# Routing of the two sparse tiles inside the expert blocks, pair lists beside the queries, packed gathers and one scan stage

## Chip, cores and metric

The kernel runs on one core of a Trainium2 chip. The metric is the device time of one execution in microseconds (us). Three runs of the kernel before took 5330.02, 5340.7 and 5357.9 us; their median is 5340.7.

## What is computed

Two layers of a decoder trunk, for 512 prompt tokens and 64 sample tokens (8 sequences of 8) that share all weights. In each layer the tokens pass a combined projection, three mixers (an RWKV-7 state, a gated delta net, a differential attention) and an output projection. Then comes the expert part, to which most of the change belongs:

```
q = (xb @ wq).reshape(TB, 8, 2, 128)
s = einsum('thcd,hcnd->thcn', q, keys)
sv, si = top_k(s, 16)
cand = sv[:, :, 0, :, None] + sv[:, :, 1, None, :]       # 16 x 16 pairs per head
tv, ti = top_k(cand, 16)                                  # 128 experts of 16384 per token
gate = softmax(tv)
act = gelu(einsum('td,tjd->tj', xb, u_tab[eidx]))
out = einsum('tj,tjd->td', gate * act, v_tab[eidx])
```

The scan that the change merges is the chunked recurrence of the two state mixers: per chunk of 64 tokens, corrections against the state, outputs, and an update of the state. The samples start from their own states, one per sequence.

## The kernel before

**Stages.** Each layer is a sequence of stages. A stage gives every engine its own list of instructions, ordered by semaphores, and ends with a barrier of all engines. All waits are written out by hand; an engine works its list strictly in order. A helper, `Steps`, counts results on a semaphore, and its `settle` (L142) waits for all of them. Tokens stand in five tiles: tile 0 (the first 128 prompt tokens), tiles 1 to 3 (the other 384) and the last tile (64 samples on 64 partitions).

**Scan (L1352 to L1410) and samples' scan (L1416 to L1487).** The prompt runs in eight chunks. In each, PE multiplies the state with 16 small products ("begins", L1365), DVE adds them into SA (L1387), PE makes the state's increment and the outputs ("ends", L1369 to L1377), and DVE scales and adds the state (L1390, L1392). Each kind of product alternates between two PSUM banks. The samples follow in a stage of their own: 128 products against their states (L1424), a turn (L1430), SA (L1465), outputs (L1435 to L1439), expansions by sequence (L1462, L1469), state increments (L1445, L1447) and additions (L1473, L1478), with a store of the states (L1483).

**Query stage (L1609 to L1699).** For each of 16 half-key lists PE makes queries and scores of all five tiles. ACT copies the scores out (L1673, L1674) into one of two buffers, and DVE takes the top 16 of each tile in five steps of five instructions (L1693 to L1697).

**Routing stage (L1732 to L1914).** The order of tiles is 0, last, 1, 2, 3. For each tile POOL adds the 16 x 16 candidates (L1829), DVE takes their top 16 for eight heads (L1859 to L1863), ACT makes the exponentials, and DVE looks up the two half indices by a comparison (L1880), a product on POOL (L1839) and a reduction (L1885). PE turns the result (L1753), ACT copies it out. Tiles 0 and last keep lists: the expert number and gate of every token and pair, for gathers ("sparse" tiles). For the 384 tokens of tiles 1 to 3 ("dense" tiles) the gates go into a table over all 16384 experts: per octet of eight tokens, DVE makes one-hots (L1849), ACT scales them (L1795), PE multiplies (L1768), ACT evicts (L1804), and SP stores the table to DRAM. One-hots of a tile are made between the steps of the next.

**Expert stage (L1966 to L2225).** It runs over 128 blocks of 128 experts. Per block: SP loads u and v (and a piece of the gate table for two blocks); ACT and DVE split u and v into two parts (L2009, L2142; L2015, L2146); PE makes hidden values of the 384 dense tokens (24 products, L153 to L155); ACT applies gelu (L2021); DVE multiplies with gates and splits (L2154 to L2160); PE multiplies with v into six PSUM banks (18 products, L2085). PE works on the hidden values of block b + 1 before the outputs of block b.

The sparse tokens ride along. POOL gathers one row of u per token and pair (`fetch_u`, L2046) into a ring of four buffers, and DVE makes a dot with the token's vector (`dot`, L2165): 128 gathers of 64 rows in blocks 0 to 39 for the samples, 128 gathers of 128 rows in blocks 40 to 82 for tile 0. Then gelu and gate, and 32 "summing" blocks each (47 to 78 and 89 to 120), in which POOL gathers rows of v (L2059), PE sums them (`half`, L2097) and DVE adds the result (L2174). The order of DVE's instructions in a block is written in the loop at the end of its list: v split of block b + 1, a dot, u split of block b + 2, a dot, the gate product of block b + 1, then the other dots.

```
LATE_DOTS, FIRST_DOTS = (0, 40), (40, 83)
LATE_SUMS, FIRST_SUMS = 47, 89
LATE_ACT, FIRST_ACT = 42, 84
```

Of the kernel before, what the change touches and what calls it, by code (L numbers as in the profile page):

```python
# [63 lines left out]
GAIN_AT = 20992  # L64
# [101 lines left out]
def trunk(nc, t):  # L166

    ctx = ExitStack()
    with ctx:
# [138 lines left out]
        with nc.Fori(0, DEPTH) as layer:  # L308
# [1043 lines left out]
            with stage(nc, "s_ready", "ws_done", "sa_ready", "out_done", "ds_done", "y_out", "scaled", "state_out", "s0_in") as (  # L1352
                    block, s_ready, ws_done, sa_ready, out_done, ds_done, y_out, scaled, state_out, s0_in):
                @block.tensor
                def _(pe):
                    for c in range(8):
                        tk = slice(c * CH, (c + 1) * CH)
                        bw, bo, bd = c % 2, 2 + c % 2, 4 + c % 2
                        at_ = lambda m, j: slice((m * 2 + j) * CH, (m * 2 + j + 1) * CH)
                        pe.wait_ge(s_ready, c + 1)  # L1360
                        if c >= 2:
                            pe.wait_ge(sa_ready, 2 * (c - 1))
                            pe.wait_ge(y_out, 2 * (c - 1))
                        for m, j, p in mh:
                            last = pe.matmul(ps[p, bw, at_(m, j)], tm(WT[m])[p, c, j], S[p, m, j], start=True, stop=True)  # L1365
                        last.then_inc(ws_done, 1)
                        pe.wait_ge(sa_ready, 2 * (c + 1))
                        for m, j, p in mh:
                            pe.matmul(ps[p, bd, at_(m, j)], tm(Kx[m])[p, c, j], SA[p, c % 2, m, j], start=True, stop=(m == 1))  # L1369
                            if m == 0:  # L1370
                                pe.matmul(ps[p, bd, at_(m, j)], tm(K_t)[p, c, j], tm(V_t)[p, c, j], start=False, stop=True)
                        for m, j, p in mh:
                            o = ps[p, bo, at_(m, j)]
# [5 lines left out]

                @block.vector  # L1380
                def _(dve):
                    dve.memset(S, 0.0).then_inc(s_ready, 1)
                    dve.wait_ge(s_ready, 1)
                    for c in range(8):
                        dve.wait_ge(ws_done, c + 1)
                        for m in range(2):
                            dve.tensor_tensor(SA[:, c % 2, m], tm(UU[m])[:, c], ps[:, c % 2, m * 128:(m + 1) * 128].rearrange("p (j n) -> p j n", j=2),  # L1387
                                              ALU.add).then_inc(sa_ready, 1)
                        dve.wait_ge(out_done, c + 1)
# [219 lines left out]
            with stage(nc, "keys_in", "wq_in0", "wq_in1", "hi_ready", "lo_ready", "q_done", "q_out", "s_done", "s_out", "v_steps", "ranked") as (  # L1609
# [15 lines left out]
                def _(pe):  # L1625
# [12 lines left out]
                    def scores(c):  # L1638
# [3 lines left out]
                        if c >= 2:  # L1642
                            pe.wait_ge(s_out, 2 * (c - 1))
# [679 lines left out]
```

## Time and profile before

| | us |
|---|---|
| median of three runs | 5340.7 |
| the profiled execution | 5362.85 |
| its span, first to last instruction | 5361.0 |
| PE busy | 4201.9 (78%) |
| DVE busy | 3266.7 (61%) |
| POOL busy | 1733.7 (32%) |
| ACT busy | 1467.0 (27%) |

The profile is of one execution. Busy shares are means over stages that have different limits, so the rows that follow later are cut by stage: layer 0 begins at 0, layer 1 at about 2695 us from the span's start. PE is TensorE, DVE VectorE, ACT ScalarE, POOL GpSimd, SP the engine that issues most DMAs; PEclk is the granted clock of PE as a part of full speed (0.50 is 1.2 GHz, 1.00 is 2.4 GHz).

### The profile page before, as it was taken

Reading aid. Unit: us, or ns where it says so; the run is one execution under the profiler, and the core shown is the slowest. Engines: PE = TensorE matmul, PEld = TensorE weight load, DVE = VectorE, ACT = ScalarE, POOL = GpSimd, SP = SyncE. Lnnn points to the kernel's source line nnn. Section 1 sums busy time; section 2 is a strip of 40 time slices with the busy share of each in tenths; the row PEclk is TensorE's granted clock in tenths of the full one; section 3 lists DMA queues with packets and bytes.
Section 4 is the critical chain, followed back from the end, with each engine's and each line's share of the span. In section 5 each row is a group of like instructions: output and inputs, shape, how many; then the busy total and the mean of one; then the engine's idle time right before and its main releaser. Section 6 shows DMA issues by size and latency. Waiting matters only on the chain. (4 is left out here: it accounts for less than half of the span.)

```text
span 5361.0 us, 79852 instructions
## 1 busy us (share of the span) xinstructions
PE 4201.9 (78%) x30618; PEld 3580.2 (67%) x30618; DVE 3266.7 (61%) x6218; ACT 1467.0 (27%) x2688; POOL 1733.7 (32%) x1020
## 2 busy tenths in 40 slices
PE   6966585814699999999978756758057999999998
PEld 6945475814688877877778545748056888778777
DVE  2064624689678878744421555247896888786444
ACT  2132201307622222222222222122075222222222
POOL 2200101222155587523222002012322545774331
PEclk9966777958899999999989667679589999999999
DMA  3120001202599999988721200011026999998885
GB/s 111 53 70 13 2 15 36 74 4 94 182 223 226 303 345 362 325 273 312 236 71 58 68 7 2 18 50 56 4 110 199 235 232 311 353 360 288 303 314 195
DMA packets 462508, 870.68 MB, mean 162 GB/s; under 512 B 224768, under 2 KB 280896, under 8 KB 458272
## 3 DMA queue, kind: packets, MB, share of 16 engines
q1 hardware_dynamic: 349600, 464.54, 28.2%
q0 software_dynamic: 112640, 402.71, 22.7%
q8 instruction: 150, 2.46, 0.2%
q14 instruction: 118, 0.97, 0.1%
HBM read 805.56 MB, written 61.58 MB: 162 GB/s over the span
## 5 line engine op out<-in xcount | busy, mean ns | idle before, releaser
L153 PE MATMUL ps<-x_split,w_split 128*128 128x384 f32 (+1 forms) x3104 | 1029.1, 332 | 117.1 <-DVE w_split L2142 66.5
L2085 PE MATMUL ps<-w_split,c_split 128*128 128x512 f32 x4608 | 1108.4, 394 | 1.0 <-DVE c_split L2160 1.0
L2085 PEld LDWEIGHTS ps<-w_split,c_split 128*128 128x128 f32 x4608 | 853.1, 188 | 277.8 <-issue 108.2
L155 PE MATMUL ps<-x_split,w_split 128*128 128x384 f32 (+1 forms) x3104 | 1008.4, 325 | 0.0
L154 PE MATMUL ps<-x_split,w_split 128*128 128x384 f32 (+1 forms) x3104 | 1007.8, 325 | 0.0
L153 PEld LDWEIGHTS ps<-x_split,w_split 128*128 128x128 f32 x3104 | 592.2, 191 | 243.1 <-issue 130.3
L2165 DVE CUSTOM_DVE_ANT_0 arena<-arena 64x1024 f32<-64x1024 f32 (+1 forms) x512 | 621.8, 1215 | 177.3 <-DMA arena<-pk_u_rows,arena 107.8
L154 PEld LDWEIGHTS ps<-x_split,w_split 128*128 128x128 f32 x3104 | 592.6, 191 | 4.0
L155 PEld LDWEIGHTS ps<-x_split,w_split 128*128 128x128 f32 x3104 | 592.0, 191 | 0.0
L2015 ACT CAST w_split<-arena 128x1024 fp32r<-128x1024 f32 x256 | 268.7, 1049 | 1080.4 <-PE ps L2085 1079.7
L2046 POOL DMA_INDIRECT arena<-pk_u_rows,arena x256 | 366.1, 1430 | 526.3 <-DVE arena L2165 352.1
L2059 POOL DMA_INDIRECT arena<-pk_v,rows_sb x256 | 263.7, 1030 | 505.2 <-PE ps L2097 441.8
L329 POOL TENSOR_TENSOR w_split<-arena,w_split 128x2048 fp32r<-128x2048 f32 (+1 forms) x54 | 245.7, 4555 | 532.3 <-ACT w_split L323 532.3
L2046 POOL DMA_INDIRECT arena<-pk_u_rows,rows_sb x256 | 364.8, 1425 | 152.1 <-DVE arena L2165 83.1
L2146 DVE TENSOR_TENSOR w_split<-arena,w_split 128x1024 fp32r<-128x1024 f32 x256 | 311.2, 1216 | 95.0 <-ACT w_split L2015 95.0
L1768 PE MATMUL ps<-arena 128*128 128x128 f32 x1536 | 224.8, 308 | 169.2 <-ACT arena L1795 169.0
L2174 DVE TENSOR_TENSOR x_sb<-x_sb,ps 64x512 f32<-64x512 f32 (+1 forms) x256 | 173.9, 679 | 282.1 <-PE ps L2097 282.1
L1768 PEld LDWEIGHTS ps<-arena 128*128 128x128 f32 x1536 | 206.9, 217 | 187.7 <-ACT arena L1795 187.6
L2021 ACT ACTIVATE arena<-ps 128x384 f32<-128x384 f32 x256 | 125.7, 491 | 749.8 <-PE ps L155 749.7
L1252 POOL TENSOR_TENSOR arena<-arena,cst 128x1152 f32<-128x1152 f32 x24 | 63.2, 2649 | 815.5 <-SPq L125 761.6
L153 PE MATMUL ps<-w_split,x_split 128*128 128x256 f32 x800 | 229.3, 287 | 114.6 <-POOL w_split L329 114.6
L2142 DVE TENSOR_TENSOR w_split<-arena,w_split 128x1024 fp32r<-128x1024 f32 x256 | 311.3, 1216 | 5.6 <-ACT w_split L2009 5.6
(367 smaller groups left out, 6564.2 us busy)
## 6 DMA issues: line engine op xcount, KB each, us to landing
arena<-pk_u SPq DMA_DIRECT2D x256, 512.0 KB, 8.4
arena<-pk_v SPq DMA_DIRECT2D x256, 512.0 KB, 6.5
g_scratch<-arena SPq DMA_DIRECT2D x24, 2048.0 KB, 6.3
arena<-g_scratch SPq DMA_DIRECT2D x128, 384.0 KB, 9.1
arena<-w_in SPq DMA_DIRECT2D x28, 1024.0 KB, 5.4
arena<-pk_wq SPq DMA_DIRECT2D x16, 1024.0 KB, 6.5
arena<-cache_k SPq DMA_DIRECT2D x32, 256.0 KB, 2.7
arena<-cache_v SPq DMA_DIRECT2D x32, 256.0 KB, 3.5
```

The costliest lines, as they stand in the source:

```text
L153: pe.matmul(out, lhi, rhi, start=(n == 0), stop=False)
L154: pe.matmul(out, lhi, rlo, start=False, stop=False)
L155: last = pe.matmul(out, llo, rhi, start=False, stop=(n == len(terms) - 1))
L329: pool.tensor_tensor(w_part(s, 1)[:, :, 0:width], raw[:, s, :, 0:width], w_part(s, 0)[:, :, 0:width].bitcast(F32), ALU.subtract).then_inc( ...
L1768: last = pe.matmul(ps[:, 4 + 2 * (s % 2) + k // 4, (k % 4) * P:(k % 4 + 1) * P], ABs[s][:, 0, k], ABs[s][:, 1, k], start=True, stop=True)
L2015: act.copy(vs[:, s, 0], v_raw[:, s]).then_inc(v_hi, 1)
L2046: pool.indirect_dma_start(u_got[r, n % RING], None, u_rows, bass.IndirectOffsetOnAxis(ap=rowid[i][r, j:j + 1], axis=0)).then_inc(f_u[n % R ...
L2059: pool.indirect_dma_start(v_got[:, q % 2, g], None, v_rows, bass.IndirectOffsetOnAxis(ap=rowid_t[LATE if q < 32 else 0][:, tok:tok + 1], a ...
L2085: done = pe.matmul(ps[:, 1 + 2 * j + n, :], c_of[hc], vs[:, s, hv, n * 512:(n + 1) * 512], start=first and m == 0, stop=last and m == 2, s ...
L2142: dve.tensor_tensor(us[:, s, 1], u_raw[:, s], us[:, s, 0].bitcast(F32), ALU.subtract).then_inc(u_ready, 1)
L2146: dve.tensor_tensor(vs[:, s, 1], v_raw[:, s], vs[:, s, 0].bitcast(F32), ALU.subtract).then_inc(v_ready, 1)
L2165: dve.tensor_tensor_reduce(out=u_got[r, n % RING], in0=u_got[r, n % RING], in1=near_x[i][r], scale=1.0, scalar=0.0, op0=ALU.mult, op1=ALU. ...
```

## The change

- **Scan.** The samples' stage is gone. Its PE work stands in pieces between "begins" and "ends" of chunks 1 and 3 to 7; DVE's and ACT's pieces stand in the same chunks. The prompt's products use one bank of each kind instead of two, and PE waits for ACT's copy (`y_out`) before each chunk's outputs.
- **Query stage.** Only the three dense tiles are ranked. ACT copies the raw scores of tile 0 and the last tile into a buffer that is kept (`kept`). DVE takes the top 16 pairs of the dense tiles here, one head behind, in 18 rounds instead of 16.
- **Routing stage.** Only dense tiles remain, with the exponentials, shifts and casts of all three in one instruction each. The products of the lookups are on DVE; POOL has no work in the stage. The load of the gain row moves to the expert stage's SP list.
- **Expert stage.** DVE routes the last tile in blocks 0 to 15 and tile 0 in blocks 13 to 28, one part per block after the block's own work. near_x (the sparse tokens' normalised vectors) is made in block 6. SP copies the upper half of the samples' lists and their vectors to partitions 64 to 127 (three DMAs behind the loads of blocks 18 and 19), so that 64 gathers of 128 rows serve the samples. POOL waits for both tiles' numbers and for this copy before its first gather. Dots run in blocks 30 to 48 (64) and 49 to 88 (128), sums in 55 to 86 and 95 to 126.

The diff, cut to its core:

```diff
+                    begins(0)
+                    ends(0)
+                    begins(1)
+                    s_against_states()
+                    ends(1)
+                    begins(2)
+                    ends(2)
+                    begins(3)
+                    s_turned()
+                    ends(3)
...
+                    begins(7)
+                    s_states(1)
+                    ends(7)
...
-                            act.copy(SC[:, d % 2, 0:4], ps[:, 4 + 2 * (d % 2), :].rearrange("p (i n) -> p i n", i=4)).then_inc(s_out, 1)
-                            act.copy(SC[0:SAMP, d % 2, 4], ps[0:SAMP, 5 + 2 * (d % 2), 0:P]).then_inc(s_out, 1)
+                            act.copy(SC[:, d % 2], ps[:, 4 + 2 * (d % 2), 0:3 * P].rearrange("p (i n) -> p i n", i=3)).then_inc(s_out, 1)
+                            act.copy(kept[0][:, d], ps[:, 4 + 2 * (d % 2), 3 * P:4 * P]).then_inc(s_out, 1)
+                            act.copy(kept[LATE][0:SAMP, d], ps[0:SAMP, 5 + 2 * (d % 2), 0:P]).then_inc(s_out, 1)
...
+                    for c in range(18):
+                        h = (c - 2) // 2
+                        if c < 16:
+                            dve.wait_ge(s_out, 3 * c + 1)
+                        for step in range(5):
+                            if c < 16:
+                                half_keys(c, step)
+                            if h >= 0 and step < 3:
+                                pairs(h, step + 3 * (c % 2))
                             st.settle()
...
+                    for n in range(3):
+                        if n >= 1:
+                            dve.wait_ge(t_out, n)
+                        for c in range(2):
+                            st.did(dve.tensor_tensor(look[c].rearrange("p h j a -> p (h j) a"), bc(C("iota")[:, 0:TOPK], 1, P),
+                                                     bc(TAf[:, c, n], 2, TOPK), ALU.is_equal))
+                            onehots(n - 1, 2 * c, 2)
                         st.settle()
                         for c in range(2):
+                            st.did(dve.tensor_tensor(look[c], look[c], bc(SIf[:, n, :, c], 2, TOPK), ALU.mult))
+                            onehots(n - 1, 4 + 2 * c, 2)
+                        st.settle()
                         for c in range(2):
+                            last = dve.tensor_reduce(route[:, c, n], look[c].rearrange("p h j a -> p (h j) a"), AX.X, ALU.add)
+                            if c == 0:
+                                st.did(last)
+                        last.then_inc(route_ready, 1)
+                        onehots(n - 1, 8, 8)
+                    dve.wait_ge(t_out, 3)
+                    onehots(2, 0, 16)
...
+            SPARSE = (LATE, 0)
+            ROUTE_AT = (0, 13)
+            DOTS_AT = ((30, 49), (49, 89))
+            DOTS_OF = (P // 2, P)
+            SUMS_AT = (55, 95)
+            ACT_AT = (50, 90)
...
+                    sp.wait_ge(pack_ready, 1)
+                    lower, upper = slice(0, SAMP), slice(SAMP, P)
+                    sp.dma_start(near_x[LATE][upper], near_x[LATE][lower]).then_inc(packed, 16)
+                    sp.dma_start(rowid[LATE][upper, 0:SAMP], rowid[LATE][lower, SAMP:P]).then_inc(packed, 16)
+                    sp.dma_start(near_gate[LATE][upper, 0:SAMP], near_gate[LATE][lower, SAMP:P]).then_inc(packed, 16)
...
+                            if b == ROUTE_AT[k] + 10:
+                                act.wait_ge(k_shifted, k + 1)
+                                act.activation(k_ex[rows_of[i]], k_ex[rows_of[i]], ACT.Exp).then_inc(k_exp, 1)
...
+                    pool.wait_ge(k_routed, 2)
+                    pool.wait_ge(packed, 48)
...
+                    def routing(k, part):
+                        i = SPARSE[k]
+                        r = rows_of[i]
+                        w = r.stop
+                        if part < 4:
+                            for step in range(5):
+                                for c in range(4 * part, 4 * part + 4):
+                                    best_of(kept[i][r, c], k_SV[r, c], k_SI[r, c], step)
+                                nr.settle()
+                        elif part == 4:
...
+                        elif part < 9:
+                            for step in range(5):
+                                for h in range(2 * part - 10, 2 * part - 8):
+                                    best_of(k_pairs[0][r, h], k_TV[r, h], k_TI[r, h], step)
+                                nr.settle()
...
+                            if 0 <= b - ROUTE_AT[k] <= 15:
+                                routing(k, b - ROUTE_AT[k])
```

Parts 4 to 15 of `routing`, each in its own block: the pair sums and a cast (4), the pairs' top 16, two heads a block (5 to 8), subtraction, shifts and a cast (9), the two comparisons (10), products (11), reductions and the expert numbers (12), gates (13), and the turned numbers (15). PE's loops are split at the two turns. Each gather and dot now covers all 128 partitions.

## Rows read from the trace of the kernel before

**Rows 1.** Busy time by stage: length, PE, PEld, DVE, ACT, POOL, PEclk, DMA share, GB/s

```profile
763.00:807.00 44.00, 33.47 (x320) 29.06 (x320) 9.25 (x16) 0.81 (x3) 0.00 (x0) 0.58 0.07 27
...
967.00:1107.50 140.50, 126.68 (x928) 121.95 (x928) 100.92 (x640) 35.46 (x70) 27.55 (x6) 0.95 0.17 53
1107.50:1426.00 318.50, 115.41 (x783) 105.40 (x783) 265.15 (x438) 165.77 (x491) 77.22 (x15) 0.74 0.19 81
...
1438.00:1787.00 349.00, 325.67 (x1594) 293.67 (x1594) 281.06 (x431) 95.70 (x115) 172.33 (x120) 0.98 1.02 228
1787.00:1867.00 80.00, 80.00 (x408) 72.77 (x406) 70.17 (x111) 24.65 (x30) 43.24 (x33) 1.00 0.99 327
1867.00:2217.00 350.00, 342.92 (x1603) 248.53 (x1602) 277.31 (x449) 79.71 (x96) 271.52 (x158) 1.00 0.99 355
...
3773.50:4092.00 318.50, 115.47 (x783) 105.43 (x783) 265.14 (x438) 165.77 (x491) 77.21 (x15) 0.74 0.19 81
...
4104.00:4455.00 351.00, 335.09 (x1662) 303.95 (x1663) 293.05 (x450) 99.92 (x120) 177.22 (x124) 0.98 1.00 237
```

**Rows 2.** Timeline of ACT in the expert stage: gelu of blocks in succession

```profile
1460.49 0.49 ACT L2021 ACTIVATE arena<-ps 128x384 f32<-128x384 f32 x1 [2.12 <-PE ps L155]
...
1468.80 0.49 ACT L2021 ACTIVATE arena<-ps 128x384 f32<-128x384 f32 x1 [2.13 <-PE ps L155]
...
2310.88 0.49 ACT L2021 ACTIVATE arena<-ps 128x384 f32<-128x384 f32 x1 [3.31 <-PE ps L155]
...
2321.55 0.49 ACT L2021 ACTIVATE arena<-ps 128x384 f32<-128x384 f32 x1 [3.31 <-PE ps L155]
```

**Rows 3.** Waits of DVE, 1438 to 1787 us: total us, times, longest

```profile
DVE arena L2165 <- DMA arena<-pk_u_rows,arena: 60.2, 45, 4.0
```

**Rows 4.** Timeline of the scan and the samples' scan: start, length, idle before

```profile
730.25 0.48 PE L1369 MATMUL ps<-arena 64*64 64x64 f32 x4 [0.66 <-DVE arena L1387]
...
761.45 0.42 DVE L1392 TENSOR_TENSOR S_sb<-S_sb,ps 128x256 f32<-128x256 f32 x1
...
765.04 1.29 DVE L1462 TENSOR_TENSOR arena<-arena,cst 128x512 f32<-128x512 f32 x2 [3.17 <-PEq L129]
...
802.24 0.35 SPq L1483 DMA_DIRECT2D o_state_s<-arena  x1
```

**Rows 5.** Busy time by window, inside the samples' scan

```profile
785.00:791.50 6.50, 6.50 (x79) 6.50 (x80) 0.00 (x0) 0.00 (x0) 0.00 (x0) 0.50 0.00 0
```

**Rows 6.** Timeline of DVE in the query stage: starts of two lists

```profile
1062.13 1.06 DVE L1693 MAX8 arena<-arena 128x8 f32<-128x128 f32 x5 [1.36 <-ACT arena L1674]
...
1069.95 1.06 DVE L1693 MAX8 arena<-arena 128x8 f32<-128x128 f32 x5 [1.37 <-ACT arena L1674]
```

**Rows 7.** Timeline of DVE in the routing stage, tile 1, and at its end

```profile
1186.22 2.70 DVE L1859 MAX8 arena<-arena 128x8 f32<-128x256 f32 x8
...
1201.11 0.42 DVE L1863 FIND_INDEX8 arena<-arena 128x8 uint32<-128x256 f32 x1
...
1202.49 4.49 DVE L1880 TENSOR_TENSOR arena<-cst,arena 128x2048 f32<-128x2048 f32 x2
1211.37 2.29 DVE L1885 TENSOR_REDUCE arena<-arena 128x128 f32<-128x2048 f32 x1 [4.38 <-POOL arena L1839]
...
1426.32 2.47 DVE L2186 SCALAR_TENSOR_TENSOR arena<-x_sb,small,arena 128x1024 f32<-128x1024 f32 x2 [19.68 <-PEq L129]
```

**Rows 8.** Groups of ACT, 1361 to 1419 us, the last dense tile: busy us, mean ns

```profile
L1795 ACT ACTIVATE arena<-arena 128x128 f32<-128x128 f32 x128 | 39.5, 418 | 2.8 <-DVE arena L1849 2.8
L1804 ACT COPY arena<-ps 128x512 f32<-128x512 f32 x32 | 17.4, 602 | 1.7 <-PE ps L1768 1.7
```

**Rows 9.** The page's costliest groups: the dots, busy us, mean ns

```profile
L2165 DVE CUSTOM_DVE_ANT_0 arena<-arena 64x1024 f32<-64x1024 f32 (+1 forms) x512 | 621.8, 1215 | 177.3 <-DMA arena<-pk_u_rows,arena 107.8
```

**Rows 10.** DMA issues, 1430 to 1790 us and 1790 to 1860 us: us to landing

```profile
arena<-pk_u_rows,arena POOLq DMA_INDIRECT x123, 9.2
...
arena<-pk_u_rows,rows_sb POOLq DMA_INDIRECT x22, 7.8
```

More of the change, by code:

```diff
@@ L63 @@
 NEAR_AT = 22784
-GAIN_AT = 20992
+KEPT_AT = 18176
 X_AT = 14 * SLOT + TILES * 3 * C_W
@@ L1354, in _ @@
                 @block.tensor
                 def _(pe):
-                    for c in range(8):
-                        tk = slice(c * CH, (c + 1) * CH)
[L1358 to L1366, printed above, removed]
+                    at_ = lambda m, j: slice((m * 2 + j) * CH, (m * 2 + j + 1) * CH)
@@ new lines, in _ @@
+                    begins(0)
[8 more added lines that the diff above has]
+                    ends(3)
+                    begins(4)
+                    s_outputs(0)
+                    ends(4)
+                    begins(5)
+                    s_outputs(1)
+                    ends(5)
@@ L1736, in trunk @@
                 g_saved = (g_saved0, g_saved1)
-                def of_octets(i, first, n):
-                    return range(i * P // OCT - GO + first, i * P // OCT - GO + min(first + n, octets(i))) if i not in near else ()
-                def lookup(n, c, r):
-                    return cands[n % 2 if c == 0 else 2][r]
+                PER = P // OCT
                 @block.tensor
@@ new lines, in _ @@
+                    act.wait_ge(shifted, 1)
+                    act.activation(ex, ex, ACT.Exp).then_inc(exp_done, 1)
+                    routes_out(0)
+                    for n in range(3):
+                        for m in range(PER):
+                            gated(n * PER + m)
+                            if m:
+                                evicted(n * PER + m - 1)
+                        evicted(n * PER + PER - 1)
+                        if n < 2:
+                            routes_out(n + 1)
@@ L1998, in _ @@
                     loads(1, 1)
-                    with sp.Fori(0, BLOCKS // 4 - 1) as i:
+                    sp.dma_start(near_x[0], t["ffn_row"][L].broadcast_to([P, D])).then_inc(row_in, 16)
+                    with sp.Fori(0, 4) as i:
                         for s in range(2):
                             loads(i * 2 + (2 + s), s)
+                    sp.wait_ge(pack_ready, 1)
[3 more added lines that the diff above has]
+                    sp.dma_start(near_gate[LATE][upper, 0:SAMP], near_gate[LATE][lower, SAMP:P]).then_inc(packed, 16)
+                    with sp.Fori(0, BLOCKS // 4 - 5) as i:
+                        for s in range(2):
+                            loads(i * 2 + (10 + s), s)
                 @block.scalar
```

547 lines of the change are left out of this document (282 added, 265 removed).

## The prediction

> **What bounds the kernel now.** I read three things in this order: busy time by stage, to see which engine is full where; the order of instructions at the borders of the stages that the change touches; and the block period of the expert stage, for what happens if work is put there.
>
> By stage [rows 1], layer 0: the samples' scan holds 44 us, of which PE is busy 33.5. The query stage holds 140.5 us with PE busy 126.7: PE bounds it. The routing stage holds 318.5 us with PE at 115 and DVE at 265, so DVE sets it, with ACT taking over at its end. Layer 1's routing stage is as long. In the expert stage PE is nearly full. A plain block takes 8.31 us and a block that also sums a quad of sparse tokens 10.66 to 10.67 [rows 2], set by PE. PE idles where dots run: 23.3 us in blocks 0 to 41 of layer 0 (349 less 325.7), 15.9 in layer 1, and 7.1 in the first 32 summing blocks (350 less 342.9). The wait that ends last there is the u gather, 60.2 us of DVE waiting in 45 waits [rows 3]: a dot that waits for its gather delays the next u split, which PE wants. So of the change's four parts, one shortens a stage that DVE bounds, and the others shift work among stages that PE bounds.
>
> The sum is made against the profiled execution: span 5361.0 us, 5362.85 with what lies around it. That is 22 us above the median of the three runs, 5340.7. The prediction is the median less the sum, and 22 us go into the range. A run of this kernel can tell about 0.5% (27 us) from no change.
>
> **Scan merged.** Removed per layer: a stage border and the samples' own chain. From the end of the last state update of the prompt (761.45 + 0.42) to the issue of the samples' state store at 802.24 are 40.4 us [rows 4]; 3.2 of them pass before the first work. Added: the same PE work, about 34 us (33.5 busy in [rows 1], little of it outside this), now queued on PE between the "begins" and "ends" halves of seven chunks. There PE idles 0.66 us waiting for DVE's SA [rows 4], so 6 x 0.66 = 4 us of it is covered and some 30 is not. DVE's expansions stand before waits for PE in the same chunk and are covered by the inserted PE work; the last four state additions, 2.5 us, stay at the end. New: 30 + 2.5 = 32.5 for 40.4: **-8 us**. The new wait of PE for y_out (outputs now have one bank) and for the states' load come after a whole chunk: nothing. Bounds: 0 if the covers fail, -25 if the inserted 33.5 us ran at twice the clock (17 less). On that: at 785 to 791.5 us PE was busy the whole time and yet had a granted clock of 0.50 [rows 5], the 1.2 GHz level, so denser work of this shape brought no clock there. The Trainium skill (TensorE: Matmul & The Clock Gate, "What's actually happening") says that the throttled clock is the default and that activity releases it. By that rule the filled scan would run at 2.4 GHz and give up to 25 us per layer instead of 8; the row speaks against it, and I keep 8.
>
> **Pair lists beside the queries.** Before, DVE does 25 top-8 instructions per half-key list on five tiles: 1069.95 less its idle 1.37 less 1062.13, or 6.45 us, and then waits for ACT, that is PE; the period is 7.82 us [rows 6]. After: 15 of these (0.258 each, 3.9 us) and, for each head, so every second list, 15 instructions on 256 wide. Forty of those took 1186.22 to 1201.53, 0.383 each [rows 7], so 5.7, and an addition over 768 elements of 0.9 (2048 take 2.25). That is 3.3 per list. DVE's total is 7.2, still under 7.82, so PE keeps the pace. The end grows: the last two lists come together, 2 x 0.75 more, and the last head has no cover, 6.6. **+8 us**. Bounds: +5 if the last head overlaps better, +16 if DVE's added waits make it slower than PE by 0.5 a list. ACT copies three pieces rather than two, inside its idle time.
>
> **Routing stage.** Removed: both sparse tiles, all pair top-k, and POOL's products and the waits for them (4.38 before one reduce [rows 7]). The dense lookups stay, with the products moved to DVE. Step by step: exponentials, shifts and casts for three tiles at once, 4.6 (an estimate from 128-wide operations near 0.25); first tile's lookups, 2 x 2.25 (compare) + 2 x 2.25 (product, taken like the compare) + 2 x 2.28 (reduce) = 13.5; a hand-over through PE and ACT, between 1 and 5, taken as 3. Then ACT paces: 128 scalings and 32 evictions take 39.5 + 17.4 us for 16 octets [rows 8], pipelined some 3.4 per octet. While DVE makes the next tile's six lookup operations between eight one-hots it supplies only one per 4 us (6 x 2.25 + 8 x 2.27 = 31.7), so the ninth octet starts at 34 and the tile ends at 34 + 8 x 3.4 + 3 = 64. Twice that is 128; the last tile is 2.3 + 16 x 3.4 + 3 = 60; the last store of the gate table and the border take 8. Sum 4.6 + 13.5 + 3 + 128 + 60 + 8 = 217 for 318.5: **-101 us**. Bounds: -114 if ACT never starves (58 per tile), -84 if the hand-overs take 6 more each. Gain row and near_x leave this stage at no gain: near_x, 2.47 us [rows 7], ran while the first u load was on its way.
>
> **Routing in the blocks.** Each sparse tile costs DVE per block: four blocks of 20 narrow top-8 (5.2), one of 2.6, four of 20/2 wide ones (3.8), one of 1.2, then 4.5, 4.5, 5.2, 1.2 and 0.4; near_x in block 6, 2.5. Together 115 us with the waits between steps some 10 more. DVE's own work is 3.7 us a block (70.17 busy in 9.6 blocks [rows 1], less 28.7 dots at 1.22 [rows 9]), so 29 blocks offer 29 x 4.6 = 133. It fits on the average; in the blocks of 5.2 it runs over by 0.6 to 1. The u split is made about 4.8 us before PE wants it (an estimate from the order of the block), so a backlog of that size is free: loss 3 us, between 0 and 12. Waits added: ACT for the subtraction before Exp (behind it the v and u casts; done a block earlier), PE for the row numbers before one transpose (hidden products behind it; two blocks of margin), SP for the pack (u and v loads behind it; ready when SP arrives, since SP stands three blocks later), POOL for routing and pack (only gathers behind it, first needed in block 30).
>
> **Dots.** 64 packed gathers of 128 rows replace 128 of 64 rows, in blocks 30 to 48 (3.37 a block), then 3.2 a block in 49 to 88, before 2.98. Landing takes 9.2 us for 64 rows and 7.8 for 128 [rows 10], so packing costs nothing per gather and saves 64. The blocks to 41 lose their 19.6 us of PE idle (mean of 23.3 and 15.9). The new ones: u, v, gate and 3.37 gathers are 3.01 MB a block. At 327 GB/s DMA was 0.99 busy with no PE idle, and 355 was the most sustained [rows 1]; so 8.5 to 8.9 us a block, 3 to 11 for the 19 blocks; I take 8 and 1 for the next six. Summing blocks carry 3.97 MB, 11.2 us at 355: 0.5 x 32 = 16 where 7.1 was lost. The Trainium skill (DMA: Bandwidth & Descriptors, "Where 436 GB/s comes from") puts a core's HBM side at about 358 GB/s. By that figure the 19 blocks would lose 2 rather than 8, an estimate; the rows' 327 to 355 decide. Balance: 3 + 8 + 1 + 16 = 28 for 26.7, less 3 for the first gate load, which no longer shares DMA with gathers: **-2**, between -22 and +25.
>
> Per layer -8 + 8 - 101 - 2 = -103, for two layers -206: 5340.7 - 206 = **5135 us**.
>
> **Rivals.** (a) DVE's backlog and gather waits eat the blocks: the blocks at their upper bound (27 more a layer) and the routing stage at -84 (17 more): -103 + 44 = -59 a layer, 5223. For it: 25 short steps in blocks of 8.31; against: the average fits. 0.12. (b) The scan takes the higher clock, -17 more a layer, by the rule named above: 5101. Against it stands [rows 5]. 0.10. (c) The routing stage does not give what it should: the dense tiles hand over as slowly as now. Then only the two sparse tiles leave, some -75 for the stage: 5340.7 - 2 x 77 = 5187. For it: ACT waits for one-hots at each tile already. 0.10. (d) Slower: routing instructions in the blocks take over twice the time, because each of the waits between steps costs DVE its pipeline. Price: 58 blocks x what exceeds 4.6; above 8.1 a block (computed 4.1 on average) the 206 are gone; at 8.6 the time is 5135 + 58 x 4 = 5367. Against: 25 such steps took 6.45 us with their waits [rows 6]. 0.03. Forecast as summed: 0.65.
>
> **Numbers.** Low: bounds of scan, stage and blocks combined, -30 a layer: 5075. High: to case (c) and into (a): 5205. Faster by over 0.5%: all but (d) and some mishap of measurement, 0.96; within 0.5%: 0.02; slower 0.02.
>
> **What would show it.** Right: routing stage near 217 us, query stage near 148, samples' work inside a scan of 84; blocks 0 to 28 at 8.31 with few longer ones; dots from block 30 with DVE waiting on gathers. Wrong: a routing stage over 240, block periods over 8.8 in blocks 0 to 28, query lists over 7.82.

## The result, and the profile after

The changed kernel takes 5089.2 us (median of four runs, 5086.4 to 5093.1); the kernel before, run beside it on the same chip, 5349.3 (5330.0 to 5370.2). The ratio is 0.9498, with a 95% interval of 0.9474 to 0.9522. The forecast was 5135 us, in a range of 5075 to 5205. The profiled execution spans 5091.2 us, 269.8 less than that of before, where the sum had 206.

Busy time by window, changed kernel, by stage as in [rows 1] (length, PE, PEld, DVE, ACT, POOL, PEclk, DMA share, GB/s): the scan with the samples inside, the query stage and the routing stage, in layer 0 and then in layer 1; then blocks 0 to 29, 30 to 54 and the first summing blocks of layer 0.

```profile
708.32:785.02 76.70, 59.02 (x961) 54.26 (x961) 19.91 (x50) 4.09 (x19) 0.00 (x0) 0.68 0.08 31
...
944.52:1095.39 150.87, 127.73 (x928) 122.99 (x928) 115.61 (x584) 36.36 (x86) 27.62 (x6) 0.92 0.16 50
1095.39:1303.02 207.63, 107.08 (x777) 98.22 (x777) 150.62 (x74) 163.04 (x485) 0.00 (x0) 0.87 0.29 122
...
3238.96:3314.13 75.17, 57.30 (x961) 52.46 (x961) 19.90 (x50) 4.09 (x19) 0.00 (x0) 0.72 0.09 31
3473.64:3623.07 149.43, 126.26 (x928) 121.53 (x928) 115.68 (x585) 36.37 (x86) 27.59 (x6) 0.92 0.16 50
3623.07:3830.33 207.26, 108.35 (x777) 99.46 (x777) 150.53 (x74) 162.91 (x485) 0.00 (x0) 0.86 0.29 122
...
1315.00:1563.00 248.00, 246.41 (x1245) 223.65 (x1246) 224.57 (x574) 80.44 (x97) 2.94 (x3) 1.00 0.51 153
1563.00:1770.00 207.00, 205.18 (x1034) 185.30 (x1033) 182.23 (x281) 61.34 (x75) 110.27 (x80) 1.00 0.99 349
1770.00:2040.00 270.00, 262.35 (x1219) 191.44 (x1217) 215.03 (x349) 61.82 (x75) 213.01 (x127) 0.98 0.99 357
```

The same stretches of the kernel before, the two scan stages together (layers 0 and 1) and the query stage:

```profile
711.94:807.43 95.49, 70.10 (x961) 62.97 (x961) 20.15 (x50) 4.28 (x19) 0.00 (x0) 0.59 0.07 25
967.43:1107.80 140.37, 126.60 (x928) 121.86 (x928) 100.93 (x641) 35.46 (x70) 27.57 (x7) 0.95 0.17 54
3374.82:3473.17 98.35, 72.94 (x960) 65.60 (x961) 20.15 (x49) 4.28 (x19) 0.00 (x0) 0.55 0.07 24
```

From these, and from the first gelu to the last of each expert stage, the ledger per layer (mean of both):

| part | predicted | measured |
|---|---|---|
| scan | -8 | -21.0 (-18.8, -23.2) |
| query stage | +8 | +9.8 (+10.5, +9.0) |
| routing stage, 318.5 us before | -101 | -111 |
| expert blocks, first gelu to last, with the first gate load | -2 | -16.8 (-21.8, -11.7) |
| sum | -103 | -139 |

Twice the sum is 278 us. Eight come back outside these parts: the last sums now run to block 126 and the time after the last gelu grows from 23.2 to 25.8 us, and the stages between the two layers take some more.

The routing stage by groups (busy, mean ns, idle before and what ended it), layer 0:

```profile
L1831 ACT ACTIVATE arena<-arena 128x128 f32<-128x128 f32 x384 | 118.0, 409 | 15.6 <-DVE arena L1864 15.6
L1864 DVE TENSOR_TENSOR arena<-cst,arena 128x2048 f32<-128x2048 f32 x48 | 108.0, 2287 | 23.9 <-PE ps L1814 12.0 <-ACT arena L1825 11.9
L1814 PE MATMUL ps<-arena 128*128 128x128 f32 x768 | 105.5, 296 | 74.7 <-ACT arena L1831 74.7
...
L1840 ACT COPY arena<-ps 128x512 f32<-128x512 f32 x96 | 51.9, 592 | 4.7 <-PE ps L1814 4.4 <-issue 0.2
```

PE waits for ACT's scalings alone (74.7 us), and ACT's own scalings and evictions wait for others only 20 us in all: ACT sets the stage, as forecast. One scaling takes ACT 118.0 / 384 = 0.31 us.

Gelu in the first summing blocks, timeline of ACT:

```profile
1773.71 0.49 ACT L2039 ACTIVATE arena<-ps 128x384 f32<-128x384 f32 x1 [2.13 <-PE ps L155]
1782.03 0.49 ACT L2039 ACTIVATE arena<-ps 128x384 f32<-128x384 f32 x1 [2.13 <-PE ps L155]
1799.40 0.49 ACT L2039 ACTIVATE arena<-ps 128x384 f32<-128x384 f32 x1 [10.04 <-PE ps L155]
```

The period of 8.31 [rows 2] holds, to 0.1 us, from the second block on in all but three of the first 30. Nearly all that the expert stage still loses lies in blocks 55 to 86, 19 us in layer 0 and 16 in layer 1, in a few long blocks like this one of 17.4 instead of 10.64. In fourteen traced layers whose expert stage is the same code these blocks lost 9 to 26 us, and the blocks from first gelu to last took 1213 to 1233 us: a difference of a few us between two single layers says nothing.

### The profile page after: what moved, and what is told of

Same layout as the page of the kernel before. It is cut to its first block and busy times, and to the rows that moved or that the text cites. A ratio compares the mean times of both kernels' runs of the same rounds, so it can differ in the third digit from the quotient of the medians.

```text
span 5091.2 us, 79448 instructions
## 1 busy us (share of the span) xinstructions
PE 4157.7 (82%) x30616; PEld 3540.1 (70%) x30616; DVE 3136.0 (62%) x5966; ACT 1473.9 (29%) x2720; POOL 1363.4 (27%) x862
## 5 line engine op out<-in xcount | busy, mean ns | idle before, releaser
L2197 DVE CUSTOM_DVE_ANT_0 arena<-arena 128x1024 f32<-128x1024 f32 x384 | 467.0, 1218 | 106.7 <-DMA arena<-pk_u_rows,rows_sb 81.2
L2066 POOL DMA_INDIRECT arena<-pk_u_rows,arena x128 | 174.7, 1365 | 1179.1 <-DVEq L2262 1025.7
L2066 POOL DMA_INDIRECT arena<-pk_u_rows,rows_sb x256 | 376.8, 1472 | 153.8 <-DVE arena L2197 96.1
L1814 PE MATMUL ps<-arena 128*128 128x128 f32 x1536 | 212.3, 297 | 147.8 <-ACT arena L1831 147.8
L1814 PEld LDWEIGHTS ps<-arena 128*128 128x128 f32 x1536 | 195.6, 207 | 165.1 <-ACT arena L1831 165.1
L2116 PE MATMUL ps<-arena 128*32 128x512 f32 x1536 | 275.0, 610 | 25.0 <-DVE x_sb L2270 22.5
```

The costliest lines, as they stand in the source:

```text
L1814: last = pe.matmul(ps[:, 4 + 2 * (s % 2) + k // 4, (k % 4) * P:(k % 4 + 1) * P], ABs[s][:, 0, k], ABs[s][:, 1, k], start=True, stop=True)
L2066: pool.indirect_dma_start(u_got[:, n % RING], None, u_rows, bass.IndirectOffsetOnAxis(ap=rowid[i][:, j:j + 1], axis=0)).then_inc(f_u[n % R ...
L2116: done = pe.matmul(ps[32 * g:32 * g + 32, 7, :], spread[:, s, g], v_got[:, s, g, n * 512:(n + 1) * 512], start=True, stop=True, skip_group ...
L2197: dve.tensor_tensor_reduce(out=u_got[:, n % RING], in0=u_got[:, n % RING], in1=near_x[i], scale=1.0, scalar=0.0, op0=ALU.mult, op1=ALU.add ...
```

## Experiments

All are edits of the changed kernel. Base: 5089.2 us, expert blocks 1223.7 and 1222.3 us from first gelu to last.

**The scan put back.** Edit: the two scan stages of before in place of the merged one.

> The changed kernel with the scan of before put back: the prompt's eight chunks in one stage, the samples in a stage of their own. Theory: what the two traces show between the state's memset and the next stage's first work (95.5 to 76.7 us in layer 0, 98.35 to 75.2 in layer 1) belongs to the merge, so 42 us come back: 5131 us (5125 to 5137), with both scan stages together at 95 to 98 us per layer. Rival: the merge itself is worth the 8 us per layer of the prediction and the rest came with something else (where the stage starts, the clock that the stage before leaves): 5105.

Measured: 5125.1 us (5115.4 to 5139.9), ratio to before 0.9563 (0.9528 to 0.9597). Both scan stages together take 98.4 us in each layer, at a mean granted clock of 0.55 in layer 0:

```profile
710.50:808.90 98.40, 73.00 (x960) 65.60 (x961) 20.17 (x49) 4.28 (x19) 0.00 (x0) 0.55 0.06 24
```

The merge is worth 36 us by the medians, at the lower end of the theory's range, and 45 by the scan's own windows, not 16: the theory. (The other 9 lie within what the expert blocks vary.) PE's work is the same list of products, but its busy time is 73.0 us apart and 57 to 59 merged. So 15 of the 22 us per layer are not covered idle time but a higher clock. The idle time of PE goes from 25.4 to 17.7 us, about the 8 that the prediction had.

**The wide products last.**

```diff
                     begins(6)
-                    s_states(0)
                     ends(6)
                     begins(7)
-                    s_states(1)
                     ends(7)
+                    s_states(0)
+                    s_states(1)
```

> The changed kernel with the samples' state products (512 columns each) moved from chunks 6 and 7 behind the last chunk. Theory: it is these products that bring the granted clock to 1.00 in chunks 6 and 7. Without them these chunks go back to 0.50 to 0.60 and take about 6.7 us each instead of 7.1 and 5.4 with the products inside, and the products stand bare at the end, 5 us at the higher clock and 10 at the lower: the scan grows by some 9 us a layer, 5107. Rival: the clock does not hang on them, the chunks run at 1.00 anyway (4.9 us as the first chunk) and only the idle time that the products covered comes back: 3 us a layer, 5095.

Measured: 5090.8 us (5087.5 to 5104.2), ratio 0.9501 (0.9469 to 0.9533): the rival's time. The scan took 82.7 and 76.1 us, where sixteen scans of kernels that leave it alone took 68.6 to 79.3, mean 75.7; so some 4 us more per layer, less than those scans differ among themselves. The clock did fall in the two chunks, as the theory has it, and in layer 1 too. First the changed kernel (716 to 724 us: PE on the products of 8 columns; 764 to 772: chunk 6 with the products of 512 columns), then this run (chunks 6 and 7 without them):

```profile
716.30:724.30 8.00, 8.00 (x107) 8.00 (x108) 0.00 (x0) 0.00 (x0) 0.00 (x0) 0.50 0.01 2
764.30:772.30 8.00, 7.03 (x114) 4.57 (x116) 2.68 (x7) 0.43 (x2) 0.00 (x0) 1.00 0.01 2
```

```profile
764.00:770.80 6.80, 5.13 (x101) 4.66 (x97) 2.54 (x7) 0.61 (x4) 0.00 (x0) 0.75 0.01 2
771.25:777.50 6.25, 5.11 (x82) 4.90 (x84) 2.11 (x6) 0.01 (x1) 0.00 (x0) 0.50 0.00 0
```

The clock follows these products; their place is worth little, since at the end they still find the higher clock for most of their 6.3 us.

**Fillers, four and two.** With reps 2 and then 1:

```diff
+                    def filler():
+                        for r in range(reps):
+                            for hf in range(2):
+                                p = slice(64 * hf, 64 * hf + 64)
+                                pe.matmul(ps[p, 7, :], C("id64")[p], cst[p, 0:512], start=True, stop=True)
...
                     begins(1)
+                    filler()
```

and the same behind begins(2) to begins(5). The fillers compute nothing that is used.

> The changed kernel with four more products of 64 x 512 on constants, into a bank that nothing reads, behind the state products of each of chunks 1 to 5: work that computes nothing, 1.7 us per chunk at the higher clock and 3.4 at the lower, 0.66 of it in time in which PE waits anyway. Theory: wide products keep the clock at 1.00 in chunks 1 to 5, whose products (about 42 us of them at 0.50 to 0.66) then take some 20 us less, and the fillers cost 1.1 x 5: 12 to 14 us less per layer, 5063. Rival: the clock stays at 0.50 and the fillers are bare cost, 2.8 x 5 per layer: 5117.

Measured: 5085.2 us (5078.3 to 5091.4), ratio 0.9485 (0.9455 to 0.9514), between the two and not clear of the base. The scan took 76.3 us in both layers, with PE busy 59 as without fillers, at a mean clock of 0.81.

> As the run with fillers in chunks 1 to 5, with two products of 64 x 512 per chunk instead of four (0.86 us at the higher clock, of which 0.66 lies in a wait of PE). The first run gave a granted clock of 0.96 to 1.00 through chunks 3 to 5 and a scan as long as without fillers (76.3 us): what the clock gave, the fillers took. Theory: half the filler keeps the clock as well, and costs 0.2 instead of 1.1 per chunk: a scan of 70 to 72 us, 5 us less per layer, 5080. Rival: half is too little to hold the clock, the scan stays at 74 to 77: 5089.

Measured: 5076.9 us (5072.8 to 5078.3), ratio 0.9462 (0.9439 to 0.9485), scans of 68.8 and 69.0 us: the theory. The whole scan, and two stretches in chunks 3 and 5:

```profile
705.85:774.68 68.83, 51.83 (x981) 43.67 (x981) 19.89 (x50) 4.08 (x19) 0.00 (x0) 0.84 0.10 35
727.00:735.00 8.00, 7.03 (x166) 5.68 (x163) 1.33 (x4) 0.43 (x2) 0.00 (x0) 0.91 0.01 2
751.00:759.00 8.00, 7.03 (x132) 4.86 (x130) 2.53 (x6) 0.60 (x3) 0.00 (x0) 1.00 0.01 2
```

More work on PE, and PE is busy 51.8 us instead of 57 to 59. In the sixteen scans without fillers PE idles 17.7 to 17.9 us, and all of their spread is its busy time: 50.9 us at a mean clock of 0.79 up to 61.6 at 0.65. So PE's clock sets the length of the scan. The order of work moves this clock but does not decide it alone: the same code without fillers reached 68.6 us once, as short as the two scans here.

**POOL takes scalings.** Three of an octet's eight (n), then two; PE waits for `b_pool` as well before an octet's products:

```diff
-                        for k in range(OCT):
+                        for k in range(OCT - n):
                             b = ABs[o % NAB][:, 1, k]
                             last = act.mul(b, b, routeT[:, 2, o * OCT + k:o * OCT + k + 1])
...
+                        for k in range(OCT - n, OCT):
+                            b = ABs[o % NAB][:, 1, k]
+                            last = pool.tensor_scalar(b, b, routeT[:, 2, o * OCT + k:o * OCT + k + 1], None, ALU.mult)
+                        last.then_inc(b_pool, 1)
```

> The changed kernel with three of each octet's eight scalings in the routing stage on POOL, which has no work there, instead of ACT. Theory: ACT sets the pace of the octets (3.29 us: eight scalings and two evictions), DVE is next with 2.27 a one-hot. With five scalings left ACT needs about 2.6: the last tile takes 47 us instead of 57, the first two 58 instead of 62, 18 us a layer, 5053. Rival: DVE or PE paces the octets with ACT only close behind, or POOL's scalings take longer than ACT's: no gain, 5089 or more.

Measured: 5140.4 us (5132.6 to 5146.8), ratio 0.9583 (0.9554 to 0.9613): 51 us slower, the rival's side. Groups of the stage, layer 0:

```profile
L1863 POOL TENSOR_SCALAR arena<-arena 128x128 f32<-128x128 f32 x136 | 177.0, 1323 | 90.8 <-DVE arena L1874 90.8
L1815 PE MATMUL ps<-arena 128*128 128x128 f32 x720 | 112.2, 328 | 87.5 <-POOL arena L1863 83.9 <-ACT arena L1832 3.6
```

PE's wait has gone over from ACT to POOL, whose scaling takes 1.32 us.

> The changed kernel with two of an octet's eight scalings on POOL. The run with three showed 1.32 us for one on POOL, where ACT takes 0.31, so that POOL set the pace with 4.0 us per octet and PE and DVE waited for it. Theory: with two POOL takes 2.65 and ACT 6 x 0.31 + 1.09 = 2.95, so ACT sets the pace again, at 2.95 instead of 3.29: 5 us less in the last tile and 1 to 2 in each of the others, 8 us per layer, 5073. Rival: a chain of one-hot, two POOL scalings and eight products per buffer of four holds the octets, no gain: 5089.

Measured: 5118.0 us (5113.6 to 5125.1), ratio 0.9543 (0.9508 to 0.9578): still 29 us slower than the base, so this theory fell too. POOL's scaling was 1.5 us here, and PE waited 69.5 us for POOL and 13.7 for ACT:

```profile
L1863 POOL TENSOR_SCALAR arena<-arena 128x128 f32<-128x128 f32 x96 | 142.8, 1505 | 114.0 <-DVE arena L1874 114.0
L1815 PE MATMUL ps<-arena 128*128 128x128 f32 x768 | 111.1, 308 | 83.2 <-POOL arena L1863 69.5 <-ACT arena L1832 13.7
```

Two of 1.5 and the step from the one-hot to POOL make more than ACT's 3.29 per octet; this sum was not tested by itself. Both runs agree that the scalings set the stage, and ACT is the faster place for them. A run with one on POOL was not made.

**How full DVE is in blocks 0 to 28.**

```diff
+                            if k == 0 and b < 29:
+                                for x in range(8):
+                                    dve.max_index(near_h[0].bitcast(U32)[:, 8 * x:8 * x + 8], C("iota")[:, 0:8], C("iota"))
                             if 0 <= b - ROUTE_AT[k] <= 15:
```

> The changed kernel with eight more index searches over 128 elements (0.26 us each, 2.06 together, results unused) on DVE in each of blocks 0 to 28. Theory: DVE has 8.31 - 3.7 = 4.6 us per block for routing and a free backlog of about one split's lead (4.8 us), and the routing as it stands uses this up almost wholly (DVE busy 8.06 of 8.31 in blocks 1 to 8, 0.7 us lost in each of blocks 18 and 19). So nearly all of the 29 x 2.06 = 60 us shows: by the sum of the parts 41 to 55 us per layer, 5170 to 5200. Rival: the blocks still have room, and less than a third shows: below 5130.

Measured (one run): 5177.5 us, 88 more than the base; the expert blocks take 46.5 and 41.2 us more, and blocks 20 to 23 have periods of 10.1 to 10.2 us. (Blocks 18 and 19 of that text are counted 17 and 18 below.) The theory holds: of 60 us added per layer, 50 and 48 show in blocks 1 to 29, so some 10 were free. In the changed kernel itself DVE runs over in silence: its v splits in blocks 1 to 3 start 9.04 us apart while PE keeps 8.31, because the split comes long before PE wants it.

```profile
1327.34 1.22 DVE L2179 TENSOR_TENSOR w_split<-arena,w_split 128x1024 fp32r<-128x1024 f32 x1
...
1336.38 1.23 DVE L2179 TENSOR_TENSOR w_split<-arena,w_split 128x1024 fp32r<-128x1024 f32 x1
...
1345.41 1.23 DVE L2179 TENSOR_TENSOR w_split<-arena,w_split 128x1024 fp32r<-128x1024 f32 x1
```

**Samples unpacked.** Rows of 64 partitions throughout, no copies, and:

```diff
-            DOTS_OF = (P // 2, P)
+            DOTS_OF = (P, P)
...
-                            pool.indirect_dma_start(u_got[:, n % RING], None, u_rows,
-                                                    bass.IndirectOffsetOnAxis(ap=rowid[i][:, j:j + 1], axis=0)).then_inc(f_u[n % RING], 16)
+                            r = rows_of[i]
+                            pool.indirect_dma_start(u_got[r, n % RING], None, u_rows,
+                                                    bass.IndirectOffsetOnAxis(ap=rowid[i][r, j:j + 1], axis=0)).then_inc(f_u[n % RING], 16)
```

> The changed kernel with the samples' u rows fetched as before, one token slot at a time: 128 gathers and 128 dots of 64 rows in blocks 30 to 48 instead of 64 of 128 rows, with no copies to partitions 64 to 127. Theory: a gather costs its turn of the ring of four and its dot whatever its rows are. By DVE alone 128 x 1.22 + 19 x 3.7 = 226 us stand in blocks that hold 158, 68 us more per layer; by the ring alone (9.2 landing, 1.2 dot, 0.6 to the next issue, four at a time) 128 gathers take 352 us, 194 more. So 5225 to 5480, and by the ring 5477. Rival: the bytes are the same and DMA sets the pace, so it stays at 5089.

Measured (one run): 5376.3 us. In the 19 blocks that the new order leaves to the samples' dots, unpacked rows undo the whole change: 287 us, 138 per layer in the expert blocks (1360.7 and 1361.5). It lies between DVE's bound and the ring's. Groups of DVE from 1575 to 1875 us, where blocks take 15 us:

```profile
L2189 DVE CUSTOM_DVE_ANT_0 arena<-arena 64x1024 f32<-64x1024 f32 (+1 forms) x131 | 158.5, 1221 | 70.8 <-DMA arena<-pk_u_rows,arena 70.2
```

**Dots behind the block's work.**

```diff
-                        for d in dots[0:1]:
-                            dot(*d)
...
-                        for d in dots[1:2]:
-                            dot(*d)
...
-                        for d in dots[2:]:
+                        for d in dots:
                             dot(*d)
```

> The changed kernel with all dots of a block behind the block's own work in DVE's order (after the v and u splits, the gate product and the sum of the quad) instead of between them. Theory: the 16 to 19 us per layer that blocks 55 to 88 lose come from dots whose gather is late and which hold back the splits and the sum that PE waits for; behind the block's work a late dot has the rest of a block to come in, and 10 to 14 us per layer come back: 5065. Rival: DVE works in order, the next block's splits meet the same late dot, and the gathers start later because the ring comes free later: 5089 to 5105.

Measured: 5136.4 us (5132.9 to 5152.0), ratio 0.9586 (0.9548 to 0.9624). Worse than even the rival had it: 47 us, with the expert blocks at 1248.1 and 1249.4. Blocks from 36 on lose, not only the summing ones. DVE's waits for u rows, all dots of layer 0, the changed kernel and then this run:

```profile
L2197 DVE CUSTOM_DVE_ANT_0 arena<-arena 128x1024 f32<-128x1024 f32 x192 | 233.4, 1218 | 50.3 <-DMA arena<-pk_u_rows,rows_sb 38.8 <-DMA arena<-pk_u_rows,arena 11.2
```

```profile
L2197 DVE CUSTOM_DVE_ANT_0 arena<-arena 128x1024 f32<-128x1024 f32 x192 | 228.5, 1218 | 84.1 <-DMA arena<-pk_u_rows,rows_sb 56.3 <-DMA arena<-pk_u_rows,arena 27.5
```

A dot frees a buffer, and only then POOL issues the next gather. Dots in a bunch free buffers in a bunch, and the gathers come back in one. This is read from the order of the instructions and the waits; the next run tests the buffers.

**Eight buffers.** The four more lie in strips 2 and 3 of the v buffers, which the samples' sums leave empty; before tile 0's first v rows POOL waits for the last dot. The dots read from the same list, `u_at`.

```diff
+            u_at = [u_got[:, k] for k in range(RING)] + [v_got[:, s, g] for s in range(2) for g in (2, 3)]
...
-                            if n >= RING:
-                                pool.wait_ge(dot_done, n - RING + 1)
-                            pool.indirect_dma_start(u_got[:, n % RING], None, u_rows,
+                            if n >= SLOTS:
+                                pool.wait_ge(dot_done, n - SLOTS + 1)
+                            pool.indirect_dma_start(u_at[n % SLOTS], None, u_rows,
...
+                        if q == 32:
+                            pool.wait_ge(dot_done, sum(DOTS_OF))
```

> The changed kernel with eight buffers for u rows instead of four (the four more are strips of the v buffers that the samples' sums do not use), nothing else moved. Putting the dots last made the blocks slower by 26 us a layer, with DVE waiting 140 us for gathers instead of 62. Theory: the ring of four is the limit. A gather is issued when a buffer comes free and lands 8 to 10 us later, about a block, so any unevenness in the freeing comes back as a late gather; with eight there is a second block of lead, and most of what blocks 36 to 86 lose (17 us per layer) goes: 10 to 15 less per layer, 5064. Rival: DMA itself is full in these blocks (3.97 MB per 10.64 us, 373 GB/s), a longer queue only waits longer: 5089.

(The 140 and 62 in that text count the waits twice; the rows above say 84.1 and 50.3.) Measured: 5068.8 us (5061.6 to 5072.8), ratio 0.9447 (0.9422 to 0.9471), expert blocks 1213.0 and 1210.9: 11 us less per layer, the theory. DVE's wait falls to 33.7 us:

```profile
L2201 DVE CUSTOM_DVE_ANT_0 arena<-arena 128x1024 f32<-128x1024 f32 x192 | 232.6, 1217 | 33.7 <-DMA arena<-pk_u_rows,rows_sb 33.2
```

Single blocks of 15 to 16 us remain in 58 to 84. What holds those was not tried.

**Unpacked, with eight buffers.** The two edits together.

> The samples' u rows unpacked, 128 gathers of 64 rows, with eight buffers. With four, the blocks 30 to 50 took 300 us per layer, of which DVE was busy 228 and waited 70 for gathers. Theory: the price of unpacking had two parts, DVE's 64 more dots, which stay, and the ring of four, which goes: 70 us less per layer there and some 12 less in the later blocks, 5212. Rival: the gathers wait for DMA or for POOL's issues rather than for a buffer: no more than 15 per layer, 5346.

Measured (one run): 5294.5 us, 82 less than unpacked with four, between the two. The wait for rows is gone as the theory has it, 70 us to 7.6 in 300; but 36 of them came back as waits of the gate product for its table, and the table's load now takes 17.0 us to land instead of 7.3. DVE and DMA issues from 1560 to 1860 us:

```profile
L2193 DVE CUSTOM_DVE_ANT_0 arena<-arena 64x1024 f32<-64x1024 f32 (+1 forms) x140 | 167.6, 1225 | 7.8 <-DMA arena<-pk_u_rows,arena 7.6
...
L2182 DVE TENSOR_TENSOR arena<-arena 128x384 f32<-128x384 f32 x24 | 13.2, 550 | 37.0 <-DMA arena<-g_scratch 35.7 <-ACT arena L2033 1.4
```

```profile
arena<-g_scratch SPq DMA_DIRECT2D x12, 384.0 KB, 17.0
arena<-pk_u_rows,arena POOLq DMA_INDIRECT x127, 11.2
```

So the price of 64-row gathers has at least two layers: the ring, whose removal gave 82 us, and under it DMA, with a share of 1.02 in this stretch. That DVE's 64 more dots (DVE busy 250 of 300 us) are a third is a sum that no run isolates.

**Eight buffers and two fillers.** Both edits that helped.

> The changed kernel with both edits that helped: eight buffers for u rows, and two fillers of 64 x 512 in each of chunks 1 to 5 of the scan. They lie in different stages. Theory: their gains add (20 and 12 us by medians): 5057 (5050 to 5065). Rival: one of the two gains was spread between runs (the scan took 72.6 to 76.7 us in kernels that do not touch it): 5065 to 5075.

Measured: 5063.0 us (five runs, 5060.6 to 5065.5), ratio 0.9453 (0.9429 to 0.9476); scans of 71.7 and 69.3 us, expert blocks of 1211.9 and 1219.7. It is 26 us below the changed kernel, and the runs of the two do not overlap, though their intervals against before touch. From the run with eight buffers alone it can't be told apart: of the filler's 12 us about half shows by the medians, and none by the ratios (0.9453 and 0.9447).

## Why the prediction was right, and where it was off

The forecast's case came: faster, by routing taken out of a stage that DVE bounded. By the profile the sum missed 64 us (269.8 for 206). As it was set against the median, 22 us below the profiled run, and the changed kernel's profiled run lies 4 above its own median, the forecast lies 46 too high. The scan, the routing stage and the expert blocks all gave more than forecast; no two large errors cancel.

- **What bounds the kernel.** Right. The routing stage went from DVE to ACT as its pace, and the other parts stayed on PE.
- **Scan, -8: mis-sized, -21 measured.** The step that failed is "some 30 is not" covered, priced at the lower clock because [rows 5] had PE busy throughout at 0.50. That row holds for the products it shows, and the changed kernel repeats it (716 to 724 us, above). But the merge also puts the wide products between the prompt's chunks, and there the clock rises: mean 0.68 and 0.72 where 0.59 and 0.55 stood. This is the second rival, to which I gave 0.10; it came with 13 us more per layer of its 17. By the rule named there (the Trainium skill, TensorE: Matmul & The Clock Gate, "What's actually happening") the filled scan should have risen throughout; the trace agrees for chunks 6 and 7 and not for the 8 us of dense narrow products. Such narrow products do not only fail to raise the clock: in all 24 traced layers with a merged scan (12 kernels) the 128 products of 8 columns keep PE busy throughout, and in the second half of them the granted clock is 0.50 in 21 layers and 0.51, 0.56 and 0.64 in three, although the first half had up to 1.00. So [rows 5] was a true row, but of one kind of product; the step took it for all.
- **Query stage, +8: right, +9.8.** PE still sets the lists (7.81 us), and the end grows by the last head, which has no cover.
- **Routing stage, -101: right, a little small.** The stage shrank from 318.5 to 207.5 us in both layers; how that divides among the two tiles gone, the pair lists gone and the products moved from POOL to DVE is not shown, as no run put one of them back. For the forecast's 217 these are the differences: octets of 3.29 us instead of the 3.4 taken (that gives 62 for 64 in the first two tiles and 57 for 60 in the last), a hand-over of 1.5 for 3, and a start of 3.6 for 4.6.
- **Routing in the blocks, 3: right, 1.8.** Blocks 15, 17 and 18 are longer by 0.4, 0.8 and 0.7 us, all else stays at 8.31 to 8.42. The run with eight more searches shows that the arithmetic of 4.6 us of room per block and a free backlog is the true limit, and that the change fills it but for some 10 us a layer. The rival that ended slower rested on this limit; its price per block was right, its condition did not come.
- **Dots, 9 for blocks 30 to 54: too high, 3.1 and 4.4.** I priced DMA by the 327 and 355 GB/s of [rows 1] as if they were limits (and 3.01 MB at 327 are 9.2 us, not 8.9); these blocks moved 349 and blocks 30 to 48 lost 1 and 2.5 us. The estimate by the page's figure (the Trainium skill, DMA: Bandwidth & Descriptors, "Where 436 GB/s comes from") gave 2 for them, and the trace agrees with that loss. As a limit the page's 358 GB/s does not hold here, and the measurement decides: blocks 71 to 79 of layer 1 moved 373 GB/s for 96 us, and blocks 30 to 48 of the run with eight buffers 371 for 158 us, neither losing time on the whole. The 357 of blocks 55 to 80, shown above, is a mean that takes in the long blocks.
- **Packing "costs nothing per gather and saves 64": right, and under-told.** It is the condition of the whole change, worth 138 us per layer. The step counted gathers and dots alone. [rows 1] had one thing more: with gathers of 64 rows DMA was full (a share of 1.02) at 228 GB/s, while gathers of 128 rows moved 327 and 355 at 0.99.
- **Summing blocks, 16: the number came, 19 and 16, the mechanism did not.** The step had DMA stretch every block to 11.2 us at 355 GB/s. Most of these blocks hold 10.64, stretches of them move 373, and nearly the whole loss lies in a few long blocks. Twice the buffers take 8 us of it away with the same bytes, and 3 more in blocks 30 to 54. That 16 was met is luck.
- **First gate load, -3: not seen.** No row stood behind it. The first two periods take 13.4 us after and 14.1 (layer 0) and 13.4 (layer 1) before.
- **What the dots of before cost, 19.6: mis-sized.** I counted PE's idle time (23.3 and 15.9 us). By the block periods of before the stalls in blocks 0 to 41 cost 32.6 and 22.4. The difference, 8 us per layer, is busy time of PE beyond what the same products take at full clock; the granted clock was 0.98 over this stage and is 1.00 in the first 30 blocks of the changed kernel. One such stall of the kernel before, timeline of PE, a block of 13.48 us:

```profile
1492.86 0.45 PE L153 MATMUL ps<-x_split,w_split 128*128 128x384 f32 x1 [3.36 <-DVE w_split L2142]
...
1493.75 0.52 PE L153 MATMUL ps<-x_split,w_split 128*128 128x384 f32 x1
...
1497.13 0.34 PE L153 MATMUL ps<-x_split,w_split 128*128 128x384 f32 x1
```

PE waits 3.36 us for DVE and then multiplies for 3.7 us at 0.52 a product before it is back at 0.34 (mean granted clock 0.76 from 1490 to 1496 us): 1.8 us more. The block is 5.2 us too long, and the idle column says 3.4.

## What to carry to other kernels

Price a stall of PE by the period of the block, not by its idle time, since the clock that it loses comes on top. Before work is moved under a bound engine, add up the second engine's room per period and its lead: that sum forecast both the free move and the dear one here. When gathers come late, look first at who frees their buffers, and when; here an order that spreads the frees was worth 26 us a layer and four more buffers 11, with the same bytes.

## What was not expected of the hardware

- Sixteen scans of identical code took 68.6 to 79.3 us. In the changed kernel's own trace the third and fourth 8 us of the scan had a granted clock of 0.50 and 0.59 in layer 0, and of 0.71 and 0.89 in layer 1.
- Two products of 64 x 512 that compute nothing, put into each of five chunks, made the scan 6 us shorter on average: four scans of 68.8 to 71.7 us.
- POOL takes 1.3 to 1.5 us for a scaling of 128 x 128 by a column that ACT does in 0.31.
- A row fetched in a gather of 64 rows holds a DMA engine half as long again as one in a gather of 128. Queue rows of 1563 to 1720 us of the changed kernel and of 1560 to 1860 us of the run unpacked with eight buffers (packets, MB, share of 16 engines):

```profile
q0 software_dynamic: 8676, 31.54, 52.7%
```

```profile
q0 software_dynamic: 12525, 41.87, 59.9%
```

Per packet that is 157 x 16 x 0.527 / 8676 = 0.153 us of an engine in the first and 0.230 in the second, where most gathers are of 64 rows, and the second filled DMA (a share of 1.02) at 238 GB/s where the first ran at 349. In the run unpacked with four buffers it is 0.219 (300 x 16 x 0.480 / 10538) at a share of only 0.82, so a full DMA alone is not the cause; what is, no run shows.
